# Where the on-chip buffers start: bases at multiples of 512 bytes against bases 128 and 64 bytes past them, in a one-core decoder layer

## The reference

```python
mod = (c_act @ w_ada[l] + b_ada[l]).reshape(B, N_SUBLAYERS, N_MOD, D)
h = modulate(rms_norm(x, norm_ffn1[l]), mod[:, 0, 0], mod[:, 0, 1])
x = x + 0.5 * mod[:, 0, 2][:, None, :] * swiglu(h, w_ffn1_in[l], w_ffn1_out[l])
h = modulate(rms_norm(x, norm_mix[l]), mod[:, 1, 0], mod[:, 1, 1])
u_pool, q_lat, kv_lat, k_rope, g_pool, g_mla = jnp.split(h @ w_in[l], split_pts, axis=-1)
...
merged = jax.nn.sigmoid(g_pool) * br_pool + jax.nn.sigmoid(g_mla) * br_mla
x = x + mod[:, 1, 2][:, None, :] * (merged @ w_out[l])
h = modulate(rms_norm(x, norm_ffn2[l]), mod[:, 2, 0], mod[:, 2, 1])
x = x + 0.5 * mod[:, 2, 2][:, None, :] * swiglu(h, w_ffn2_in[l], w_ffn2_out[l])
```

## Time and profile before

| | us |
|---|---|
| median of 3 runs | 1083.03 |
| lowest, highest | 1080.96, 1083.68 |
| profiled execution, its own time | 1080.96 |
| its span, first to last instruction | 1079.1 |
| TensorE busy in the span | 1047.2 |
| VectorE, ScalarE, GpSimd busy | 530.8, 370.0, 70.0 |

### The profile page before, as it was taken

The page is one execution under the profiler, slowest core; times in us unless marked ns, Lnnn a source line. Parts: engine busy times, 40 slices in busy tenths (PEclk is TensorE's granted clock), DMA queues, the critical chain, the costliest instruction groups (busy, mean ns, idle before and its releaser), DMA issues.

```text
span 1079.1 us, 13106 instructions
## 1 busy us (share of the span) xinstructions
PE 1047.2 (97%) x5086; PEld 882.0 (82%) x5086; DVE 530.8 (49%) x718; ACT 370.0 (34%) x519; POOL 70.0 (6%) x56
## 2 busy tenths in 40 slices
PE   3999999999999999998999999999999999999998
PEld 2888888888888899896888887898888888888887
DVE  5765555554663284688565555474232333322221
ACT  6533232323212143575444443333232323222211
POOL 0000000000000000851000004200000000000000
PEclk9999999999999999998999999999999999999999
DMA  9864545454763322131121122322323232222222
GB/s 360 306 244 166 216 173 208 181 194 159 260 234 113 121 82 101 71 105 52 40 78 53 64 78 79 118 79 79 117 78 117 78 112 83 92 81 85 102 87 97
DMA packets 28878, 138.62 MB, mean 128 GB/s; under 512 B 3248, under 2 KB 3504, under 8 KB 21168
## 3 DMA queue, kind: packets, MB, share of 16 engines
q1 hardware_dynamic: 28848, 138.23, 35.5%
HBM read 136.12 MB, written 2.10 MB: 128 GB/s over the span
## 4 chain that ended last, share of the span: by engine, by line
PE 86%; DVE 6%; POOL 3%; ACT 2%; issue 1%; DMA 1%; SPq 1%; DVEq 0%; POOLq 0%; ACTq 0%
PE bank L450 28%; PE bank L451 27%; PE bank L452 27%; PE bank L794 2%; POOL window L1947 1%; DMA ada_first<-w_ada 1%; DVE w_lo L1290 1%; ACT w_hi L894 1%; PE bank L810 1%; DVE qk_tok L1533 1%; POOL u_pad L1953 1%; POOL window L1952 1%; PE bank L776 1%; POOL h L1976 0%; DVE mvar L1639 0%
## 5 line engine op out<-in xcount | busy, mean ns | idle before, releaser
L450 PE MATMUL bank<-h_hi,w_hi 128*128 128x512 f32 (+1 forms) x976 | 373.2, 382 | 3.3 <-DVE h_lo L1480 2.5
L451 PE MATMUL bank<-h_hi,w_lo 128*128 128x512 f32 (+1 forms) x976 | 370.4, 379 | 0.0
L452 PE MATMUL bank<-h_lo,w_hi 128*128 128x512 f32 (+1 forms) x976 | 370.2, 379 | 0.0
L1290 DVE TENSOR_TENSOR w_lo<-w_raw,w_hi 128x2048 fp32r<-128x2048 f32 (+3 forms) x94 | 192.9, 2052 | 159.8 <-ACT w_hi L894 159.8
L450 PEld LDWEIGHTS bank<-h_hi,w_hi 128*128 128x128 f32 x976 | 184.1, 189 | 40.5 <-DVE h_lo L1480 2.9
L452 PEld LDWEIGHTS bank<-h_lo,w_hi 128*128 128x128 f32 x976 | 183.9, 188 | 34.9
L451 PEld LDWEIGHTS bank<-h_hi,w_lo 128*128 128x128 f32 x976 | 184.1, 189 | 33.5
L894 ACT ACTIVATE w_hi<-w_raw 128x2048 fp32r<-128x2048 f32 (+3 forms) x94 | 160.9, 1712 | 114.1 <-PE bank L452 63.8
L450 PE MATMUL bank<-act_hi,w_hi 128*128 128x512 f32 (+1 forms) x374 | 141.2, 377 | 0.5 <-DVE w_lo L1290 0.5
L451 PE MATMUL bank<-act_hi,w_lo 128*128 128x512 f32 (+1 forms) x374 | 140.8, 376 | 0.0
L452 PE MATMUL bank<-act_lo,w_hi 128*128 128x512 f32 (+1 forms) x374 | 140.8, 376 | 0.0
(11 more groups left out here) (189 smaller groups left out, 906.1 us busy)
## 6 DMA issues: line engine op xcount, KB each, us to landing
w_raw<-w_ffn_in SPq DMA_DIRECT2D x41, 1024.0 KB, 4.8
ada_raw<-w_ada SPq DMA_DIRECT2D x56, 512.0 KB, 5.2
w_raw<-w_ffn_out SPq DMA_DIRECT2D x32, 704.0 KB, 4.0
w_raw<-w_mix SPq DMA_DIRECT2D x19, 1024.0 KB, 4.8
ada_first<-w_ada SPq DMA_DIRECT2D x16, 512.0 KB, 12.2
w_raw<-w_ffn_in SPq DMA_DIRECT2D x6, 512.0 KB, 12.4
w_raw<-w_mix SPq DMA_DIRECT2D x3, 896.0 KB, 4.5
x_tok<-x_rows SPq DMA_DIRECT2D x4, 512.0 KB, 6.5
```

Source lines behind the costliest of these rows:

```text
L450: nc.tensor.matmul(dst, a_hi, b_hi, start=start, stop=False)
L451: nc.tensor.matmul(dst, a_lo, b_hi, start=False, stop=False)
L452: return nc.tensor.matmul(dst, a_hi, b_lo, start=False, stop=stop)
L1290: nc.vector.tensor_tensor(w_lo[slot][:, 0:size], w_raw[slot][:, 0:size], w_hi[slot][:, 0:size].bitcast(F32), ALU.subtract).then_inc(lo_don ...
```

## The change

The first buffer starts at 16512 in place of 16896, which is 384 bytes lower. `phase_at` is no longer rounded up to a multiple of 512, which takes another 64 bytes off everything behind it.

```diff
     with ctx:
-        cursor = [16896]
+        cursor = [16512]
 
         def place(name, shape, dt=F32, at=None):
...
         ssq = place("ssq", [P, S])
-        cursor[0] = (cursor[0] + 2048 + 511) // 512 * 512
+        cursor[0] += 2048
         phase_at = cursor[0]
```

## The result

| | us |
|---|---|
| before, median of 5 runs | 1082.81 (1080.96 to 1083.68) |
| after, median of 5 runs | 1088.89 (1088.32 to 1090.45) |
| ratio after / before, 95% interval | 1.0064, 1.0052 to 1.0077 |
| span of the profiled execution, before and after | 1079.1 and 1088.0 |

The prediction forecast no change, 1083.0 us. The kernel became slower by 6.1 us, nearly twice the 3.2 us that it called the least that can be told. The result lies inside its wide range of 1079.5 to 1092 us, but on the side to which it gave 0.37. All times of the layer in this text are of undisturbed executions; only the first run with the stage buffers alone at 64 had others, two of its four, at 2142.68 and 3768.93 us.

What follows compares the result with a forecast made beforehand. It took TensorE's matmul count times start distance as the bound. All parts were priced 0: 1080.96 + 0 = 1080.96 us, plus 2.07 us to the median, giving 1083.0 us; 8-in-10 range 1079.5 to 1092 us.

Steps and rivals of the forecast that it cites:

- the side to which it gave 0.37: Whole kernel slower past 0.3%, by a slower moved operand or an unseen VectorE or ScalarE cost; chance 0.37.
- What bounds the kernel: TensorE, busy 97% of the span: the time is a number of matmuls times the distance between two starts.
- The weight load: Stationary operands on TensorE: sums of squares take 110 ns at either offset, so the new offsets cost 0.
- The moved operand: Reads of `h` and `act` in 4050 matmuls: taken as 0, bounded between 0 and 20.3 us.
- upper bound of 5.0 ns: Slower read that the weight load could hide in a 224-column matmul (111.7 against 106.7 ns); times 4050, 20.3 us.
- The argument from 64-byte pieces: Moved reads: both shifts are multiples of 64 bytes, so a 2048-byte read has as many pieces as before; cost 0.
- A gain is excluded: Moved reads on TensorE: aligned ones show no scatter to remove, and no 224-column offset goes under 110 ns.
- The first rival: Products of `h` and `act` read more slowly off a multiple of 512: 1089.9 us, at most 1103.3; within a shared 0.37.
- Its test: Second feed-forward block: 228 ns or more between `h` or `act` starts shows slower reads; one alone moving identifies the offset.
- VectorE and ScalarE, 0: Their instructions at shifted offsets: no cost, as durations differ by at most 2%; if all grew 2%, 1.7 us.
- DMA, 0, with a rival at +0.6 us: Start's DMAs: no cost, or 3.4% of 18.4 us, giving 1083.8 us with the last store; inside no change's 0.55.
- The rival of a collision that goes away: Mixer waits or engine collisions vanish with the stage buffers' new distance: 3.5 us less, 1079.5 us; faster past 0.3% had 0.08.

## Why the prediction was wrong, point by point

**What bounds the kernel** was right: a number of matmuls times the distance of their starts, and the whole change went through that distance.

**The weight load, priced at 0.** As far as its row went this holds: `ssq` at 448 loaded as fast as `sq_last` at 0. But the row moved one column, and so had hardly a moved read for the load to meet. The cost is in the pair, and no one-sided row can show it.

**The moved operand, "I take 0".** This is the step that failed. The price was 6.7 ns for each of 990 matmuls and 0 for each of 2640, where the prediction had one price for 4050 (420 of which move 256 columns). Its upper bound of 5.0 ns was too low as well. It was built by carrying what 224-column rows could hide over to 512 columns, as a constant a matmul. The runs show that the cost isn't one: at a difference of 192 it is 6.7 ns with 512 columns, 1.5 ns with 384, and -2.4 ns with 256. The 224-column reads passed through 0, 384, 256 and 128 against stationary `h` at 0. Modulo 256 these are only 0 and 128; the difference that the change made, 192, has no row at all. And the 2.68 us for 24 didn't tell whether 512 columns would feel even 128. The argument from 64-byte pieces was beside the point: both shifts were multiples of 64, and the difference between them, 64, was what did the damage. "A gain is excluded" was wrong for 256 columns, where 120.0 ns became 117.7.

**The first rival** had the side and nearly the time, 1089.9 us, but not the mechanism. That the time fits is luck: 1.7 ns for 4050 matmuls is 6.9 us, and 6.7 ns for 990 is 6.6. "Off a multiple of 512" would have charged the 2640 `h` matmuls too; they kept 226.9 ns. Its test ("if only one of the two moves, the offset that matters is known") pointed at the right rows and drew too much from them: 64 as such is harmless, as the kernel with everything at 192 shows.

**VectorE and ScalarE, 0.** Right: 598 and 693 ns, beside 598 and 692 before.

**DMA, 0, with a rival at +0.6 us.** The profiled execution shows the first product 0.9 us later and 403 in place of 415 GB/s, 3% less. The prediction's row for `c_wide` had bounded it at 3.4%. An estimate from the Trainium skill ("DMA: Bandwidth & Descriptors", section "How a descriptor splits into AXI transactions") was 6%. The page speaks of where a descriptor starts and of bytes fetched, and what moved here is the place that is written; the trace shows half of the 6%. The kernels with these places at 128 and at 192 have 404 and 403 GB/s between 9 and 30 us, and their medians are 0.9 us above and 0.1 us below before. But the boundary alone doesn't do it: in the two kernels with `x` at 128, the weights at 192 and the stage buffers at a multiple of 512 the engines moved 416 and 414 GB/s, and in the two profiles with the stage buffers alone at 64, 413 and 409. So this part is of the size forecast, its cause isn't shown, and it can't be told in the device time.

**The rival of a collision that goes away.** Something of it is there, too small to show in the time. TensorE's waits of the mixer for `h_lo` and `qk_tok` shrank, in all by 1.8 us. Those of the kernel before (us in total, times, longest), of which the first two are 4.1 and 0.3 us in the changed one and the last is gone:

```profile
PE bank L776 <- DVE qk_tok L1533: 4.7, 1, 4.7
...
PE bank L450 <- DVE h_lo L1533: 0.8, 1, 0.8
PE bank L450 <- DVE h_lo L1366: 0.7, 2, 0.4
```

The slower matmuls ahead of them, the 3.4 us at half clock above all, can explain that, and then it is no gain. The 132 half matmuls of `act` did get faster, by 0.3 us in sum.

**What stays open.** Why a difference of 0 modulo 256 is the fast one: the runs show that the weight load is one side and that with 32 stationary columns the effect is gone, and no run shows which part of the memory the two meet in. Of the 0.8 us in the first up phase 0.7 fall in its first 48 matmuls, while the DMAs of the start still land. In the mixer 96 `attn` products at some 6 ns cost 0.6 us and the 224-column matmuls, by the stretch at half clock, 0.5 us; against these stand the shorter waits. Whether the change has to do with that stretch is open: two of the other kernels have one near 395 us too, with `h` at 128 and at 64 against weights at 0, and the rest have none.

## What to carry to other kernels

Where matmuls of 512 columns with full weight loads of 128 columns run back to back on 4-byte operands, which is the case measured here, place stationary and moving operands at the same offset modulo 256 bytes; which of 0, 64, 128 and 192 it is doesn't matter. An allocator that rounds each region on its own, or not at all, can break this with small tensors between two regions, so look at the distance between matmul starts by pair of tiles, not by line, and where one shape has two paces at the same granted clock, think of the addresses. A price taken from rows that touch one side only, or from another shape, isn't a bound for a pair.

## What the runs showed that I had not expected

The pace of a matmul depends on the relation of two addresses: 226.7, 228.9, 232.4 and 233.4 ns for differences of 0, 64, 128 and 192 modulo 256, and 236.7 ns for a moving operand 4 bytes past against 0, 240.0 against 64. With 256 columns a difference of 0 is the slowest of the four, 120.1 ns against 117.8 to 118.7. The pace settles only over some ten matmuls after a change of operands, so short groups may keep the marks of what ran before them. I take this to be why the attention's 24 products of `p` and `v` with 512 columns, three at a time after products of `h`, took 230.9 ns in the changed kernel, at a difference of 0, where they took 226.7 before; no run tests it.
